# Down projections of four feed-forward networks by seven products per 2x2 square of weight tiles

## The reference, cut to what matters

```python
def conv_ffn(x, w_up, conv_w, conv_b, w_down):
    u = causal_depthwise_conv(x @ w_up.astype(x.dtype), conv_w, conv_b)
    g, val = jnp.split(u, [FFN_DIM], axis=-1)          # FFN_DIM = 3072
    return (jax.nn.gelu(g) * val) @ w_down.astype(x.dtype)
...
    hf = rms_norm_2(x, g_ffn)
    x = x + jnp.square(jax.nn.relu(hf @ w_up)) @ w_down    # 4096 hidden channels
```

## Time and profile before

| | |
|---|---|
| median of 3 runs | 2782.74 us (2782.54 to 2783.49) |
| the profiled execution, its span | 2781.7 us |
| matmuls | 12993 |
| PE, DVE, ACT, POOL busy | 99%, 45%, 45%, 44% |
| slabs loaded | 470 of 512 KB |

### The profile page before, as it was taken

The page is one execution under the profiler, slowest core; times in us unless marked ns, Lnnn a source line. Parts: engine busy times, 40 slices in busy tenths (PEclk is TensorE's granted clock), DMA queues, the critical chain, the costliest instruction groups (busy, mean ns, idle before and its releaser), DMA issues.

```text
span 2781.7 us, 32569 instructions
## 1 busy us (share of the span) xinstructions
PE 2765.4 (99%) x12993; PEld 2261.2 (81%) x12993; DVE 1256.4 (45%) x2112; ACT 1246.5 (45%) x1823; POOL 1225.9 (44%) x545
## 2 busy tenths in 40 slices
PE   9999999999999999999999999999999999999999
PEld 8876888888888888887778888888877778888887
DVE  4676551544675525337666432021266674420112
ACT  4665442444864334334774343143345844442332
POOL 4222444444554444443455444444434564444443
PEclk9999999999999999999999999999999999999999
DMA  4222333333333323332222333333332223333332
GB/s 153 92 69 61 92 100 97 99 98 98 91 98 92 105 91 99 98 100 88 72 76 84 99 99 99 93 96 99 106 92 75 63 91 93 97 99 99 95 95 83
DMA packets 75879, 259.27 MB, mean 93 GB/s; under 512 B 9984, under 2 KB 12032, under 8 KB 75728
## 3 DMA queue, kind: packets, MB, share of 16 engines
q1 hardware_dynamic: 74432, 256.13, 29.9%
q10 hardware_dynamic: 1296, 1.05, 0.1%
HBM read 254.95 MB, written 2.13 MB: 92 GB/s over the span
## 4 chain that ended last, share of the span: by engine, by line
PE 95%; DVE 2%; ACT 1%; issue 1%; DMA 0%; POOL 0%; SPq 0%; DVEq 0%; ACTq 0%
PE ps L470 28%; PE ps L471 28%; PE ps L472 28%; PE ps L546 2%; PE ps L577 2%; PE ps L560 1%; PE ps L603 1%; PE ps L604 1%; PE ps L605 1%; PE ps L526 1%; PE ps L527 1%; PE ps L528 1%; ACT pbuf L1070 0%; PE ps L481 0%; ACT w_hi L1010 0%
## 5 line engine op out<-in xcount | busy, mean ns | idle before, releaser
L2182 POOL TENSOR_TENSOR w_lo<-raw,w_hi 128x1024 fp32r<-128x1024 f32 x469 | 1131.0, 2414 | 1476.2 <-ACT w_hi L1010 1476.0
L470 PE MATMUL ps<-xs,w_hi 128*128 128x512 f32 x2176 | 859.4, 395 | 1.6 <-DVE xs L1529 1.6
L471 PE MATMUL ps<-xs,w_hi 128*128 128x512 f32 x2176 | 847.1, 389 | 0.0
L472 PE MATMUL ps<-xs,w_lo 128*128 128x512 f32 x2176 | 847.0, 389 | 0.0
L1010 ACT ACTIVATE w_hi<-raw 128x1024 fp32r<-128x1024 f32 x470 | 494.6, 1054 | 626.5 <-PE ps L472 589.7
L470 PE MATMUL ps<-hid,w_hi 128*128 128x512 f32 x1300 | 508.3, 391 | 0.0
L472 PE MATMUL ps<-hid,w_lo 128*128 128x512 f32 x1300 | 506.0, 389 | 0.0
L471 PE MATMUL ps<-hid,w_hi 128*128 128x512 f32 x1300 | 505.9, 389 | 0.0
L470 PEld LDWEIGHTS ps<-xs,w_hi 128*128 128x128 f32 x2176 | 408.6, 188 | 95.5 <-issue 7.8
L471 PEld LDWEIGHTS ps<-xs,w_hi 128*128 128x128 f32 x2176 | 408.7, 188 | 87.1 <-issue 3.8
L472 PEld LDWEIGHTS ps<-xs,w_lo 128*128 128x128 f32 x2176 | 408.5, 188 | 85.6
(11 more groups left out here) (249 smaller groups left out, 2625.7 us busy)
## 6 DMA issues: line engine op xcount, KB each, us to landing
raw<-in_weights SPq DMA_DIRECT2D x470, 512.0 KB, 3.5
btab<-in_rel SPq DMA_DIRECT2D x8, 256.0 KB, 3.8
hT<-in_x SPq DMA_DIRECT2D x3, 512.0 KB, 7.1
btab<-in_heads SPq DMA_DIRECT2D x6, 256.0 KB, 4.0
tmp<-in_heads SPq DMA_DIRECT2D x6, 256.0 KB, 4.0
out<-tmp SPq DMA_DIRECT2D x8, 128.0 KB, 1.8
out<-tmp ACTq DMA_DIRECT2D x8, 128.0 KB, 1.8
common<-in_fixed SPq DMA_DIRECT2D x1, 642.0 KB, 10.6
```

Of the source, the lines that this page charges most:

```text
L470: pe.matmul(banks[bank][:], wh, rh, start=(k == 0), stop=False)
L471: pe.matmul(banks[bank][:], wh, rl, start=False, stop=False)
L472: last = pe.matmul(banks[bank][:], wl, rh, start=False, stop=(k == len(specs) - 1))
L2182: gp.tensor_tensor(w_lo[:, n % NPAIR, :], raw[:, n % NRAW, :], w_hi[:, n % NPAIR, :].bitcast(F32), ALU.subtract).then_inc(*w_low.tick(n))
```

## The change

The down products of a part are made by a form of Strassen's algorithm. A part now has eight hidden tiles (three parts in `network`, four in `hybrid` 0, two in `hybrid` 1, whose third part keeps 16 hidden tiles and the old form). The eight hidden tiles form four pairs, the eight output tiles four pairs, in two groups g of two (p). For a pair of hidden and a pair of output tiles, a 2x2 square, the tokens are also halved (256 each), and seven products of one 128x128 weight operand with a 128x256 activation operand replace the eight of the ordinary way. The weight operands are A11, A12, A22 as loaded, and S1 to S4, sums that VectorE makes of whole slabs (`slab_sums`, into tiles of pt). Each of the seven has a slab of its own, split as before, in the order A11, S1, A12, S2, S4, S3, A22; four slabs are loaded per group. The activation operands are the first half of the even tile (A11), T1 (S1), the two halves of the odd tile (A12, S4), and T2, T3, T4 (S2, S3, A22): VectorE makes T1 for an even tile, the others for an odd one (`pair_low`), and their high and low parts are made with those of the halves (`pair_high`). The products lie in three regions for each p, six banks; A12 follows on A11's region, S4 on S1's, S3 and A22 on S2's, and each waits until VectorE has read out the region. `group_sums` adds each region to the tiles of hT that it belongs to: 14 operations of 256 columns and two of 512 for a group. With six buffers for loaded slabs during networks (the three further ones in pbuf), `angles` works in tmp.

```diff
 BIG = 1e30
+PRODUCTS = ("a11", "s1", "a12", "s2", "s4", "s3", "a22")
+REGION = {"a11": 0, "s1": 1, "s2": 2, "a12": 0, "s3": 2, "s4": 1, "a22": 2}
+OPERAND = {"a11": 0, "s1": 1, "a12": 2, "s4": 3, "s2": 4, "s3": 5, "a22": 6}
 LOG1P = [2.0 / (2 * i + 1) for i in range(9)]
...
+        def put_group(key, name, layer, c0, k0):
+            close_slab()
+            n11, n21, n22, n12 = (new_raw() for i in range(4))
+            for n, k1, f in ((n11, 0, 0), (n21, 0, 1), (n22, 1, 1), (n12, 1, 0)):
+                for p in range(2):
+                    for i in range(4):
+                        c = c0 + P * (2 * p + f)
+                        pieces.append((n, P * (4 * p + i), P, (name, (layer,), P * (k0 + 2 * i + k1), [(c, c + P)])))
+            parts = {"a11": ("raw", n11), "s1": ("sum", 0), "s2": ("sum", 1), "a12": ("raw", n12), "s3": ("sum", 2),
+                     "s4": ("sum", 3), "a22": ("raw", n22)}
+            for m in PRODUCTS:
+                w = place[key, m] = new_split(parts[m])
+                opens[(key, m), 0] = [w]
+                if m[0] == "s":
+                    i = parts[m][1]
+                    sum_of[w] = (key, m, {"s1": (n21, n22), "s2": (None, n11), "s3": (n11, n21), "s4": (None, n12)}[m])
+                    sum_before[w], last_in_sum[i] = last_in_sum[i], w
+            freed[n11] = [(w_low, place[key, "a11"]), (added, (key, "s3"))]
+            freed[n21] = [(added, (key, "s3"))]
+            freed[n22] = [(added, (key, "s1")), (w_low, place[key, "a22"])]
+            freed[n12] = [(w_low, place[key, "a12"]), (added, (key, "s4"))]
...
+        def pair_parts(i):
+            return hid_flat[:, 3584 * i:3584 * i + 1792], hid_flat[:, 3584 * i + 1792:3584 * i + 3584]
+        extra = tmp[:, 0:2, :].rearrange("p a b -> p (a b)")[:, 0:768]
...
+            def group_of_products(key, name, layer, c0, k0, inner):
...
+                    put_group(key, name, layer, c0, k0)
+                kind, L = key[0], key[1]
+                for m in PRODUCTS:
+                    w, q = place[key, m], OPERAND[m]
+                    T.wait_ge(w_low, w)
+                    for p in range(2):
+                        bank = 3 * p + REGION[m]
+                        o = banks[bank][:, 0:256]
+                        if m in ("a11", "s1", "s2"):
+                            wait_bank(bank)
+                        elif m == "a12":
+                            T.wait_ge(resid, (key, "a11", p))
+                        elif m == "s3":
+                            T.wait_ge(resid, (key, "s2", p))
+                        elif m == "s4":
+                            T.wait_ge(resid, (key, "s1", p))
+                        else:
+                            T.wait_ge(resid, (key, "s3", p))
+                        for i in range(4):
+                            c = inner + 2 * i
+                            if q < 2:
+                                T.wait_ge(low, ("hid_a", kind, L, c))
+                            elif q < 4:
+                                T.wait_ge(low, ("hid_b", kind, L, c + 1))
+                            else:
+                                T.wait_ge(low, ("hid_e", kind, L, c + 1))
+                            at = P * (4 * p + i)
+                            wh, wl = w_hi[:, w % NPAIR, at:at + P], w_lo[:, w % NPAIR, at:at + P]
+                            rh, rl = (part[:, 256 * q:256 * q + 256] for part in pair_parts(i))
+                            first = m in ("a11", "s1", "s2") and i == 0
+                            more = m not in ("a11", "s1", "s2")
...
-                for part in range(2):
-                    for c in range(12 * part, 12 * part + 12):
+                at_slab["ring"], at_slab["since"] = WIDE, len(raw_slot)
+                at_slab["guard"] = [] if L else [(turned, ("first", 31, 0))]
...
+                    for g in range(2):
+                        group_of_products(("down", L, part, g), "ffn_w_down", L, 512 * g, 8 * part, 8 * part)
+                at_slab["ring"] = NRAW
...
+                if kind == "raw":
+                    A.wait_ge(l_slab[raw_slot[i]], i)
+                else:
+                    A.wait_ge(added, sum_of[n][0:2])
                 if n >= NPAIR:
...
-                ac.activation(w_hi[:, n % NPAIR, :], raw[:, n % NRAW, :], ACT.Copy).then_inc(*w_high.tick(n))
+                ac.activation(w_hi[:, n % NPAIR, :], whole(n), ACT.Copy).then_inc(*w_high.tick(n))
...
+            def pair_high(kind, L, c, b, before):
+                if before is not None:
+                    A.wait_ge(product, before)
+                parts = pair_parts(c % 8 // 2)[0]
+                if c % 2 == 0:
+                    A.wait_ge(vec, ("t1", kind, L, c))
+                    take_high(parts[:, 0:512], b, ("hid_a", kind, L, c))
+                else:
+                    A.wait_ge(vec, ("t2", kind, L, c))
+                    take_high(parts[:, 512:1024], b, ("hid_b", kind, L, c))
+                    A.wait_ge(vec, ("t4", kind, L, c))
+                    take_high(parts[:, 1024:1792], extra, ("hid_e", kind, L, c))
+            def group_weights(key, m=None, between=None):
+                for f in PRODUCTS:
+                    weights((key, f))
+                    if between and f in between:
+                        between[f]()
+                    if m is not None and key[3] and f in PRODUCTS[2:6]:
+                        square_chunk(m, PRODUCTS.index(f) - 2)
+                if m is not None and key[3]:
+                    for c in range(4, 8):
...
+            def slab_sums(upto):
+                while sums_done["n"] < min(upto, len(sources)):
+                    w = sums_done["n"]
+                    sums_done["n"] += 1
+                    if w not in sum_of:
+                        continue
+                    key, f, raws = sum_of[w]
+                    for n in raws:
+                        if n is not None:
+                            V.wait_ge(l_slab[raw_slot[n]], n)
+                    if sum_before[w] is not None:
+                        V.wait_ge(w_low, sum_before[w])
+                    if f in ("s2", "s4"):
+                        V.wait_ge(added, (key, "s1" if f == "s2" else "s2"))
+                    a, b = (sum_slots[sources[w][1] // 2 if n is None else 0] if n is None else raw_slots[raw_slot[n]] for n in raws)
+                    ve.tensor_tensor(whole(w), a, b, ALU.add).then_inc(*added.tick((key, f)))
+            def sums_for(group):
+                slab_sums(opens[group, 0][-1] + NPAIR + 1)
+            def pair_low(kind, L, c, b, other):
+                hi, lo = pair_parts(c % 8 // 2)
+                first, second = slice(0, 256), slice(256, 512)
+                if c % 2 == 0:
+                    ve.tensor_tensor(b[:, second], b[:, first], b[:, second], ALU.subtract).then_inc(
+                        *vec.tick(("t1", kind, L, c)))
+                    V.wait_ge(vec, ("t1", kind, L, c))
+                    take_low((hi[:, 0:512], lo[:, 0:512]), b, ("hid_a", kind, L, c))
+                else:
+                    t2 = extra[:, 0:256]
+                    ve.scalar_tensor_tensor(out=t2, in0=other[:, second], scalar=-1.0, in1=b[:, second], op0=ALU.mult,
+                                            op1=ALU.subtract).then_inc(*vec.tick(("t2", kind, L, c)))
+                    V.wait_ge(vec, ("t2", kind, L, c))
+                    ve.scalar_tensor_tensor(out=extra[:, 256:512], in0=t2, scalar=-1.0, in1=other[:, first], op0=ALU.mult,
+                                            op1=ALU.subtract).then_inc(*vec.tick(("t3", kind, L, c)))
+                    ve.scalar_tensor_tensor(out=extra[:, 512:768], in0=t2, scalar=-1.0, in1=b[:, first], op0=ALU.mult,
+                                            op1=ALU.subtract).then_inc(*vec.tick(("t4", kind, L, c)))
+                    take_low((hi[:, 512:1024], lo[:, 512:1024]), b, ("hid_b", kind, L, c))
+                    V.wait_ge(vec, ("t4", kind, L, c))
+                    take_low((hi[:, 1024:1792], lo[:, 1024:1792]), extra, ("hid_e", kind, L, c))
+            def group_sums(key, m=None):
...
+                g = key[3]
+                def onto(o, cols, bank, op, *events):
+                    V.wait_ge(resid, last_sum[o])
+                    wide = cols == slice(0, S)
+                    dst = hT[:, o, cols].rearrange("p (a b) -> p a b", b=256) if wide else hT[:, o, cols]
+                    src = banks[bank][:, 0:256].unsqueeze(1).to_broadcast([P, 2, 256]) if wide else banks[bank][:, 0:256]
+                    ve.tensor_tensor(dst, dst, src, op).then_inc(*resid.tick(*events))
+                    last_sum[o] = events[0]
+                for f in PRODUCTS:
+                    sums_for((key, f))
+                    for p in range(2):
+                        o1, o2, bank = 4 * g + 2 * p, 4 * g + 2 * p + 1, 3 * p + REGION[f]
+                        V.wait_ge(product, (key, f, p))
+                        if f == "a11":
```

(39 more changed lines are left out.)

191 lines of the change are left out of this document (123 added, 68 removed).

## The result

The kernel after takes 2851.03 us (median of 4 runs, 2850.50 to 2853.89) where the kernel before took 2783.11 on the same chip: 1.0248 times as long, 95% interval 1.0233 to 1.0262. The prediction was 2863 us, range 2794 to 2895. The profiled execution of after spans 2849.2 us against 2781.7 of before, 67.5 us more, with a granted clock of 0.986 on average.

The account below looks back on a forecast made before the run. TensorE's matmuls were taken to bound the kernel before; 2781.7 - 38.5 (matmuls) + 46 (network parts) + 32 (hybrid parts) + 30 (last groups) + 10.5 (softplus, angles) = 2861.7, forecast as 2863 us, range 2794 to 2895.

Parts of the forecast that it names:

- Matmuls: Down products on TensorE: 0.20 us saved per 2x2 square, 192 squares, 38.5 us less if nothing waits.
- Start of a part, networks: Network down parts: A12's late split makes TensorE wait 5.2 us; part 48.1 against 40.3 unstalled, 46 us for six.
- Hybrid parts: Hybrid down parts: shorter hidden-tile chain, S3 starts at 18.3, part 45.7 us; 5.3 us each, 32 us for six.
- A steady group at 21.6 us: Steady down groups: splits, sums and read-outs hold A22, so the period is 21.6 us against 21.76 before, returning the saving.
- the claim that the group has no room: Per down group: GpSimd's splits and VectorE's sums add up to 21.0 to 21.7 us, over TensorE's 20.16.
- Last groups: Last group of networks 0, 1 and hybrid 0: chunks alternate with splits, A22 starts 7.5 us late; 10 us each, 30 us.
- Softplus and angles: Between last hidden tile and group read-outs: 5 and 5.5 us on the path, 10.5 us (ends 5 and 20).
- Parts at nothing: Up phases, weight DMAs, tmp ring waits and angles moved to tmp: put at no cost.
- The rival of the clock: TensorE's waits halve its clock; a dozen waits cost 31 us less what splits catch up: 2870 to 2895. Chance 0.13.
- The rival that sums don't hold GpSimd: Slab sums leave GpSimd's splits alone; parts wait only for A12, 4.1 us in networks, 1.6 in hybrids: 2795. Chance 0.14.
- Faster: Part-start waits vanish since A12's split is there by 5.76 us: full saving 2744, likelier 2760 to 2775. Chance 0.09.

Follow-up runs that it names:

- experiment 4: Kernel after, with 14 (networks 18) dummy matmuls of 512 columns into a free bank ahead of TensorE's wait for A12: 2849.1 us.
- experiment 12: After, with ScalarE staging one sum operand in PSUM (S4, S3 copies early), softplus and angles behind, chunks spread, squares of chunks 2 to 7 in PSUM: 2825.43 us.
- experiment 8: After, with first-group sums, A12's w_hi and A11's read-outs earlier, softplus and angles later, other hidden-tile banks, chunks reordered, last groups' squares in PSUM: 2838.65 us.
- 7: After, with first-group sums during up products, A12's w_hi and A11's read-outs earlier, softplus and angles behind first part's products, hidden tiles in other banks: 2848.17 us.
- experiment 3: Kernel after, with softplus and angles behind the second group of the first part: 2836.28 us.
- experiment 1: Kernel after, with each slab sum adding a PSUM bank to one slab, leaving out one summand: 2820.9 us.
- 10: After, with sums staged through PSUM by ScalarE, A12's w_hi and A11's read-outs earlier, softplus and angles later, other hidden-tile banks, chunks spread: 2878.9 us.
- 11: After, with A12's w_hi and A11's read-outs earlier, softplus and angles later, other hidden-tile banks, chunks reordered, last groups' squares in PSUM; sums unmoved: 2851.51 us.
- 2: Kernel after, with ScalarE copying A12's w_hi right behind the gelu or square of the part's last hidden tile: 2868.31 us.
- 5: Kernel after, with all four slab sums of each part's first group made during the up products: 2885.44 us.

## Right and wrong, point by point

- **Matmuls: right.** 4032 half products, 0.12 us apart, and the whole saving of 38.4 us is there in the ledger: 2781.7 - 38.4 + 106.1 = 2849.4, span 2849.2.
- **Start of a part, networks: the size right, its make-up in part luck.** Predicted 7.7 us a part, measured 7.03 on the mean of the two middle parts (47.95, 46.75), 42 us for six against 46. The 7.7 were 6.3 for the start (S3 at 20.7 in place of 14.4) and 1.4 for a first group that runs at 21.6; measured, the 7.03 are all start. The wait for A12 was predicted as 5.2 us and is 4.4 to 4.95 from start to start; w_hi of A12 behind the extra columns in ScalarE's queue, and its split held by the S2 sum, are as written (3.39 us).
- **Hybrid parts: the number right by luck.** 5.3 us a part, 32 us, measured 5.30 on the mean of the five parts without chunks. But the 5.3 were 3.9 for the start and 1.4 for the period of 21.6, which did not come. A12's wait is 3.4 net and not 2.7, and the rest is slow steps, which the sum had at nothing (1.5 us a part), and in two parts 0.7 at S1 for its split. Over the twelve parts, 17 us too much for the period and some 13 too little for the starts cancelled.
- **A steady group at 21.6 us: wrong.** No part shows a wait in its second group unless chunks are in it, and of the waits for A22's bank in a first group one is left, 0.49 us (387.93), beside one step of 0.28 in `network` 1's first part. The step that failed is the place of A22's split, put to end 2.45 us after S3's start, with the next S1 sum waiting it out until 3.5. In the hybrid part above S3 starts at 1835.40, the split had begun at 1834.13 and ended 1.13 after S3's start, and the sum, issued at 1835.94 as written, was over 2.2 us after S3's start; A22 started on time at 1838.28. GpSimd was that far ahead, it seems, because TensorE had stood still for it at A12; with TensorE at full clock (experiment 4) the same split ends 1.7 after S3's start. Sums of the second group of a hybrid part take 1.68, 1.63, 1.51 and 2.58 us and the seven splits 20.2 us in all, 3.4 more than the 16.8 of seven alone. So a sum costs GpSimd some 0.8 us and not the predicted 1.05 to 1.23, and the demand is 20.2 and not 21.0 to 21.7, just what TensorE takes (20.16). With GpSimd at 19.24 of 20 us the claim that the group has no room was near the truth: in experiment 4, at full clock, A22 waits 0.49 us at this very place, in experiment 12 1.46.
- **Waits missed.** The first products need banks that the last up product's taps still read: 2.0 us at A11's second half in the networks' first parts, 0.7 at S1 in the middle ones (VectorE's tmp in the table of waits, 4.3 us in all). The first parts of both hybrids wait 0.8 at S1 for its split. They come ahead of the wait for A12 and mostly out of it.
- **Last groups: mechanism right, size half too large again.** Predicted 30 us, measured 4.5 + 7.3 + 8.4 = 20.2 (each last part less an ordinary one of its network). The chunks' operations do go in turn with splits (2.18 to 2.89 us each) and A22 is late; it is late by 3.9, 3.9 and 6.2 us and not 7.5, and the 2 to 3 us behind the part did not occur. With turns taken away the last parts are 15.3 us shorter (experiment 8 against 7) and 16.5 (experiment 12 against after).
- **Softplus and angles: right in kind, somewhat small.** 10.5 us predicted, 12.2 by the parts, 14.8 by experiment 3.
- **Parts at nothing: right.** Outside the twelve parts the two kernels agree to 0.2 us.
- **The rival of the clock: the mechanism is there, its price is not.** The clock falls behind the waits, some 295 steps cost 0.09 us more each, 27 us by counting, 31 in the prediction. Taking away 13 us of them by counting won 1.9 at most (experiment 4). The step that failed in this rival was to add them to the sum: where GpSimd bounds the stretch, slow products cover its lateness. Where it does not, they count in full, 1.47 us in a part of experiment 1.
- **The rival that sums don't hold GpSimd: refuted** by experiment 1, 30.1 us. GpSimd's busy time rose by 241.9 us (1225.9 to 1467.8) and not by the predicted 173, since a split that is held counts as busy; in experiment 1 it rose by 176.5. The prediction's estimate of 1.23 us for a sum alone is 1.22 in the trace.
- **Faster: refuted.** A12's split would have to be ready when it is wanted. Experiments 10 and 11 brought it nearly there, and the time went to S2.

The total came out 12 us below the forecast because the last groups were put 10 us too high and the network parts 4, against 2 too low for softplus and angles; that it is not further off is in part the cancelling of the period against the starts. What stays open: how much of the last groups is the chunks' low part (L1683) and how much the sum of squares (L1700). Experiment 8 eased only the second, but with a new order of the chunks beside it, and no kernel changed the first. Nor was the start of a part tried with less work for the last hidden tile. Of the 106.1 us over the unstalled length, removal has shown 30.1 for the turns and 14.8 for softplus and angles; that most of the rest is A12's wait behind the last hidden tile's work is read from the order of time, and no edit took that wait away without another coming in its place.

## What to carry to other kernels

Fewer multiplications pay only if the engines that feed them have room: here 7.4% less TensorE time per square came with 75% more splits, and GpSimd went to 19.24 of 20 us. Before you make a product shorter, write down what each other engine does per product and which of it shares a path; then look at the first product behind every phase change, where the look-ahead is spent and the late tile's work is still queued. When a wait is pulled forward in one queue, ask whose work it displaces: the edits of experiments 2, 5, 10 and 11 moved the wait to another product or another releaser, and the gain in experiment 12 came from softplus and angles out of the way and from turns taken out of the last groups. Slow steps behind a wait can be counted, but what they cost depends on whether another engine is late in the same stretch.

## What the runs showed of the hardware

- The turns work both ways. A 1.22 us slab sum that starts 0.05 us ahead of a split makes the split 3.39 us; a sum issued behind a split took up to 2.85. With one input in PSUM, the same width took 1.21 us, and 96 splits beside 96 such sums kept 2403 ns. The Trainium skill (SBUF — State Buffer, Who interferes with whom) says that a VectorE instruction with two SBUF inputs contends with a GpSimd one that reads SBUF; both runs agree.
- At the lower level 256 columns take 0.213 us (median of some 300 steps) against 0.120, a factor of 1.78, not 2: the 13 ns that a matmul costs beside its columns at 2.4 GHz don't show at 1.2.
- ScalarE copies 512 columns from SBUF into PSUM in 0.58 us (583 ns mean over 192), shorter than a VectorE addition of that width with one input there (682 ns).
